# Residual steps at the end of four stages: last three weight pieces by token halves, and both residual halves ahead of the next splits

## What is computed

```
# block 1
mixed = (g_conv * y_conv + g_attn * y_attn) @ w_o
x = x + gt1 * rms_norm(mixed, g_post_mix)              # end of stage "w_o"
h = rms_norm(x, g_pre_ffn) * (1 + sc2) + sh2
f = (silu(h @ w_gate) * (h @ w_up)) @ w_down
x = x + gt2 * rms_norm(f, g_post_ffn)                  # end of stage "w_down"
# block 2
proj = rms_norm(x, norm_mix_pre) @ w_in_2 ...
x = x + rms_norm(concat(a, c) @ w_out_2, norm_mix_post)  # end of stage "w_out_2"
hn = rms_norm(x, norm_ffn_pre)
f = (silu(hn @ w_gate_2) * (hn @ w_up_2)) @ w_down_2
x = x + rms_norm(f, norm_ffn_post)                     # end of stage "w_down_2", the output
```

## Time and profile before

| | us |
|---|---|
| time, median of 3 runs | 2622.82 |
| lowest and highest of them | 2622.46, 2627.53 |
| the profiled execution, its own time | 2625.36 |
| its span, first to last instruction | 2623.6 |
| TensorE busy | 2570.8 (98% of the span) |
| DVE busy | 1688.5 (64%) |
| ACT busy | 1278.8 (49%) |
| mean granted TensorE clock | 0.995 of full speed |

### The profile page before, as it was taken

The page is one execution under the profiler, slowest core; times in us unless marked ns, Lnnn a source line. Parts: engine busy times, 40 slices in busy tenths (PEclk is TensorE's granted clock), DMA queues, the critical chain, the costliest instruction groups (busy, mean ns, idle before and its releaser), DMA issues.

```text
span 2623.6 us, 28987 instructions
## 1 busy us (share of the span) xinstructions
PE 2570.8 (98%) x11654; PEld 2101.7 (80%) x11654; DVE 1688.5 (64%) x1937; ACT 1278.8 (49%) x1775; POOL 3.9 (0%) x11
## 2 busy tenths in 40 slices
PE   7999999999999999999999999999999999999998
PEld 5788778878878888888888787788788888888886
DVE  7999899989875555555555645666655454445455
ACT  4445677754454444444444545554544444444443
POOL 0000000000000000000000000000000000000000
PEclk9999999999999999999999999999999999999999
DMA  9998466877946556666555454445455555555553
GB/s 373 358 350 311 156 222 211 292 285 287 372 182 214 206 215 240 240 225 225 202 199 185 169 191 162 171 167 195 166 194 184 191 208 191 193 188 184 190 192 129
DMA packets 80425, 578.14 MB, mean 220 GB/s; under 512 B 8974, under 2 KB 8982, under 8 KB 10529
## 3 DMA queue, kind: packets, MB, share of 16 engines
q1 hardware_dynamic: 78768, 566.92, 59.3%
q10 hardware_dynamic: 1010, 6.67, 0.6%
q0 software_dynamic: 512, 2.69, 0.3%
HBM read 574.13 MB, written 3.68 MB: 220 GB/s over the span
## 4 chain that ended last, share of the span: by engine, by line
PE 87%; DVE 5%; ACT 3%; DMA 3%; issue 1%; DVEq 0%; ACTq 0%; SPq 0%
PE bank L688 83%; DVE wlo L1528 2%; DMA raw<-in_w_o 1%; PE bank L640 1%; ACT whi L1013 1%; DMA raw<-in_w_in 1%; DVE X L1523 1%; DVE raw L1538 1%; PE bank L800 0%; ACT SS L1189 0%; PE bank L726 0%; PE bank L783 0%; PE bank L934 0%; DVE SC L1685 0%; PE bank L848 0%
## 5 line engine op out<-in xcount | busy, mean ns | idle before, releaser
L1528 DVE TENSOR_TENSOR wlo<-raw,whi 128x1024 fp32r<-128x1024 f32 x882 | 1074.2, 1224 | 882.6 <-ACT whi L1013 879.3
L1013 ACT ACTIVATE whi<-raw 128x1024 fp32r<-128x1024 f32 x882 | 931.0, 1058 | 1248.5 <-PE bank L688 1118.7
L688 PE MATMUL bank<-whi,HTh 128*128 128x512 f32 x2560 | 703.8, 397 | 7.9 <-ACT HTh L1013 5.9
L688 PE MATMUL bank<-wlo,HTh 128*128 128x512 f32 x2560 | 687.7, 390 | 5.9 <-DVE wlo L1528 5.9
L688 PE MATMUL bank<-whi,HTl 128*128 128x512 f32 x2560 | 689.0, 391 | 0.1
L688 PEld LDWEIGHTS bank<-wlo,HTh 128*128 128x128 f32 x2560 | 480.8, 188 | 110.0 <-DVE wlo L1528 8.7
L688 PEld LDWEIGHTS bank<-whi,HTl 128*128 128x128 f32 x2560 | 482.2, 189 | 104.7 <-DVE HTl L1523 1.3
L688 PEld LDWEIGHTS bank<-whi,HTh 128*128 128x128 f32 x2560 | 471.6, 189 | 106.6 <-issue 10.6
L1538 DVE CUSTOM_DVE_ANT_0 raw<-raw,GT,VECS 128x2048 f32<-128x2048 f32 x96 | 225.0, 2347 | 2.5 <-DMA raw<-in_w_ada 2.5
L688 PE MATMUL bank<-whi,ACTh 128*128 128x512 f32 x704 | 192.3, 394 | 0.0
L688 PE MATMUL bank<-wlo,ACTh 128*128 128x512 f32 x704 | 190.4, 391 | 0.0
(11 more groups left out here) (227 smaller groups left out, 1198.7 us busy)
## 6 DMA issues: line engine op xcount, KB each, us to landing
raw<-in_w_in SPq DMA_DIRECT2D x128, 1024.0 KB, 4.9
raw<-in_w_ada SPq DMA_DIRECT2D x96, 1024.0 KB, 6.5
raw<-in_w_gate SPq DMA_DIRECT2D x88, 1024.0 KB, 4.8
raw<-in_w_up SPq DMA_DIRECT2D x88, 1024.0 KB, 4.8
raw<-in_w_down SPq DMA_DIRECT2D x88, 1024.0 KB, 4.8
raw<-in_w_o SPq DMA_DIRECT2D x16, 1024.0 KB, 7.2
raw<-in_w_out SPq DMA_DIRECT2D x16, 1024.0 KB, 4.8
raw<-in_w_attn_out SPq DMA_DIRECT2D x8, 1024.0 KB, 4.8
```

Of the source, the lines that this page charges most:

```text
L688: i = e.matmul(bank[2 * ch.st + t][:, :], (xl if ps == 1 else xh)[:, k, tk(t)], (lo if ps == 2 else hi)[:, j * 512:j * 512 + 512], start=c ...
L1013: return e.activation(dst, src, ACT.Copy, scale=scale)
L1528: e.tensor_tensor(lo, src, r32(hi), S_).then_inc(lo_done, 1)
```

## The change

1. TensorE does the last three pieces of each of the four stages by token halves: half 0 of L-2, L-1 and L (then `pe_t0`), half 1 of L-2, L-1 and L, each of the last three with its `pe_done`.
2. ACT does residual half 0 in slot L-1, ahead of rounding L+1, and residual half 1 in slot L, ahead of rounding L+2.
3. DVE does both residual halves in slot L-1, ahead of subtraction L+1. All three subtractions L+1, L+2 and L+3 now stand between residual half 1 and the next norm.
4. For n = 0, half 1: ACT takes half 0's second root ahead of squaring half 1's columns, and DVE makes half 0's diagonal and the multiplication with the gain row ahead of the mean, where the mean came first. The list of DVE's steps is put in that order.

```
@@ order of DVE's steps, n = 0 @@
-    ... "quad0", (0, 0), "sum1", "mean1", "minv0", "dg0", "inv1", ...
+    ... "quad0", (0, 0), "minv0", "dg0", "sum1", "mean1", "inv1", ...
@@ tensor, piece(s) @@
-            if ch.apart and s == ch.p1 - 1:
+            if ch.apart and ch.p1 - 2 <= s < ch.p1:
                 half(s, 0)
                 return
             if ch.apart and s == ch.p1:
                 half(s, 0).then_inc(pe_t0, 1)
-                half(s - 1, 1).then_inc(pe_done, 1)
-                half(s, 1).then_inc(pe_done, 1)
+                for d in (2, 1, 0):
+                    half(s - d, 1).then_inc(pe_done, 1)
                 return
@@ scalar, residual(n, t) @@
-            evict(aparts[n], (t,))
             if n == 0 and t:
                 root(0, rr_mod[:, 0:1], res_dve[0]("quad0"), "mroot0")
+            evict(aparts[n], (t,))
@@ scalar, slots @@
+            if s + 1 in last_of:
+                residual(last_of[s + 1], 0)
             if s in last_of:
-                residual(last_of[s], 0)
-            if s - 1 in last_of:
-                residual(last_of[s - 1], 1)
+                residual(last_of[s], 1)
@@ vector, residual(n, t) @@
-            mean(n, rr, n, t, sq_act[n](3, t), "")
-            if t == 0 or n == 0:
-                late(n, t)
             if (n, t) == (0, 1):
                 diagonal(0)
+                late(n, t)
+            mean(n, rr, n, t, sq_act[n](3, t), "")
+            if t == 0:
+                late(n, t)
@@ vector, slots @@
-            if s in last_of:
-                residual(last_of[s], 0)
-            if s - 1 in last_of:
-                residual(last_of[s - 1], 1)
+            if s + 1 in last_of:
+                for t in R(2):
+                    residual(last_of[s + 1], t)
```

More of the change, by code:

```diff
@@ L434, in build @@
     JT = QT
-    res_dve = [steps("res0_dve", ["sum0", "mean0", "inv0", "xsum0", "msum0", "lin0", "quad0", (0, 0), "sum1", "mean1",
-                                  "minv0", "dg0", "inv1", "xsum1", "msum1", "lin1", "quad1", (0, 1), "minv1", "dg1",
+    res_dve = [steps("res0_dve", ["sum0", "mean0", "inv0", "xsum0", "msum0", "lin0", "quad0", (0, 0), "minv0", "dg0",
+                                  "sum1", "mean1", "inv1", "xsum1", "msum1", "lin1", "quad1", (0, 1), "minv1", "dg1",
                                   *QT[2:]])]
```

## The result

The changed kernel takes 2631.89 us (median of 8 runs, 2629.2 to 2634.47), the kernel before 2625.08 in the same comparison (8 runs, 2621.38 to 2627.53). The ratio is 1.0026, with a 95% interval of 1.0018 to 1.0035: **slower by 6.8 us**. The prediction had +6.0 us, but put it on the first three runs of before (2622.82) and not on a base that eight runs put 2.3 higher; the time lies 0.09 us above the range.

What follows compares the result with a forecast made beforehand. The bound was DVE, working in its given order, finishing the first `HTl` at the stage ends. Terms 1.25 + 0.6 + 2.3 - 0.45 = +3.7 us, plus +2.3 for the clock, gave +6.0, 2628.8 us; range 2625.3 to 2631.8.

Steps and rivals of the forecast that it cites:

- the median of the three runs is 2.54 lower, and I put the difference on the median: Base of the forecast: differences taken against the profiled 2625.36 us, then put on the three runs' median, 2.54 lower.
- The sum of the change, +6.0: Whole kernel: +3.7 us from DVE's order plus +2.3 us from the clock; as the summed case, chance 0.50.
- The order, +3.7: DVE's order at the four stage ends: `w_o` +1.25, `w_down` +0.6, `w_out_2` +2.3, `w_down_2` -0.45 us.
- 1.25 later: At `w_o`, three subtractions ahead of `HTl` instead of one make `HTl` 1.25 us later.
- the "0" for the chain up to the addition: At `w_o`, L's later end and the removed subtraction cancel up to residual half 1's addition: 0, with 0.3 either side.
- The clock, +2.3: New stall puts off the clock's return: last two passes at half speed at `w_o` and `w_out_2`, together +2.3 us.
- the upper bound of 5.1: Upper bound of the clock term, +5.1 us: the next piece too is slow in two places, 1.4 each.
- a new stall between the passes puts the return off: At the first three ends, stalls of 1.2, 1.9 and 1.8 us between first and second pass could delay the clock's return.
- Case B: Rival: the clock comes back where it did, only DVE's order costs, +3.7 us, 2626.5; chance 0.33.
- Case C: Rival: the subtractions are no cost, only gains remain, -2.2 us, 2620.6, or 2618.7 with the clock early; chance 0.07.
- Case D: Rival: half 0 not early at `w_down` and `w_down_2`, +0.5 in each; 2632 with slow next pieces; chance 0.10.
- What would show it: Signs: two more subtractions before `HTl`, its release 1.2, 0.6, 2.3 later, line 1633 behind TensorE's end, clock 0.50 throughout L+1.

Runs made afterwards that it cites:

- order_only: The changed kernel with TensorE's edit taken back, so only the last two pieces by token halves: 2630.77 us, +5.3 us against before.
- low_between: The changed kernel, but DVE takes subtraction L+1 between the two residual halves: 2627.89 us, +3.9 us against before.
- lows_behind: The changed kernel, with DVE's subtractions L+2 and L+3 behind the first quarter of the next norm: 2623.08 us, ratio 0.9994 to before.
- before_l3_behind: The kernel before, with DVE's subtraction L+3 alone moved behind the first quarter of the next norm: 2623.64 us, ratio 0.9993.
- the filled kernels: after_filled and before_filled: the changed kernel and the kernel before, with extra matmuls where TensorE would wait; +0.5 and -0.3 us against before.
- after_fill_t: The changed kernel with eight extra matmuls between the two halves' transposes only, at each of the first three ends: 2629.99 us, +5.0 us against before.
- after_filled: The changed kernel with extra unused matmuls, eight between the halves' transposes and seven between L+1's first and second pass: 2626.49 us, +0.5 us against before.
- before_filled: The kernel before with extra unused matmuls, eight between the halves' transposes and three between the passes: 2624.97 us, -0.3 us against before.

## Why the prediction was right or wrong

**The time** fell out of the range by 0.09 us. The step that failed is "the median of the three runs is 2.54 lower, and I put the difference on the median". Eight runs of before have a median of 2625.08, within 0.3 of the profiled execution's 2625.36; with three runs spread over 5 us the base was uncertain by 2 us, and the range, 3.5 down and 3.0 up from the forecast, held none of that. On a base of 2625.08 the same sum gives 2631.1, and the same range takes in 2631.89. The sum of the change, +6.0, against +6.8 measured (4.7 to 9.2 by the interval), stood. That it came so near is in part luck, for its larger term was too large, and something else made up for it.

**The order, +3.7, was too large.** By the traces it is +0.55, +0.36, +2.05 and -0.4, together 2.5. At `w_o` "1.25 later" was 0.55: three subtractions in a row take 3.49 us, not 3.67, and residual half 1's chain was 0.3 shorter than I had it; the "0" for the chain up to the addition was in truth a gain. At `w_down` and `w_out_2` the 0.2 of the three subtractions is nearly the whole miss. The mechanism held at each place: two more subtractions between addition and `HTl`, the release by DVE, `HTh` not what is waited for, `pe_t0` at `w_o` held by the wait for the weights (1.23 against 1.22 us before). order_only, low_between and lows_behind each moved one thing and moved the gap as this reading says, within 0.4 us at `w_down` and `w_out_2`; before_l3_behind did not at `w_down`, where the first pass at 1.2 GHz was the limit. The Trainium skill, page "TensorE: Matmul & The Clock Gate", section "Architectural detail: the array is 16× 32×32, not 1× 128×128", says that ACT and DVE are strict FIFO. The traces agree: in the changed kernel the subtractions of L+2 and L+3, which no pass of L+1 needs, are done ahead of the `HTl` for which TensorE stands.

**The clock, +2.3,** is neither confirmed nor refuted in its size. What the order leaves of the total is 4.3 us (2.2 to 6.7 by the interval); the filled kernels give 3.8 to 6.0, uncertain by some 3.5; the mean granted clock leaves room for 2.9, give or take 2.6. In this one pair of executions the last two passes took only 0.3 longer in all. I had costed eight matmuls at half speed at two ends, and nothing at `w_down`, because the one execution before showed all eight slow there already. But the clock varies from one execution to the next: its mean lies between 0.991 and 0.995 in the eight of the changed kernel, and one profile shows one draw of it. Whether the upper bound of 5.1 holds is open too. The reasoning, that a new stall between the passes puts the return off, held at two of three ends: counted from the start of the second pass, the clock came back after 4.4 us at `w_down` (4.0 in the kernel before) and after 3.0 at `w_out_2` (1.3 in the kernel before), but at `w_o` it was back ahead of that pass (in the kernel before 1.1 behind its start). With the sentence of the Trainium skill, page "TensorE: Matmul & The Clock Gate", Part 1, that I set beside it, "the default state is throttled, and activity releases the throttle", the trace agrees at those two ends. after_fill_t shows what the prediction did not have: the new wait can also bring the fall itself.

**The rivals.** Case B (the order alone): its +3.7 is below the interval, and the order alone is by the traces no more than 2.5; after_filled wins 6.3 us with all gaps as they were. Case C: the subtractions are a cost, in every trace. Case D: half 0 was early where it was said to be. At `w_down` its sum (line 1633) ran at 1475.90, 4.1 us ahead of TensorE's end, where it had run 2.7 ahead, and L's weights were there in time. **What would show it**: of the signs named, the release by DVE, line 1633 behind TensorE's end and the two more subtractions came; the clock was at 0.50 throughout both passes at `w_down`, mostly at `w_out_2`, but not at `w_o`.

What is still open: how large the clock's part is within some 2 to 5 us, and how it divides over the three ends, which would need many profiled executions of each kernel.

## What to carry to other kernels

Count what stands ahead of the instruction that the idle engine waits for, in the order of the engine that gives it; work that is not needed for some us goes behind it, and work that can run in a wait stays in the wait. When TensorE has to stand, a wait inside its first busy stretch can cost more than its length, for what follows may run at 1.2 GHz (in after_fill_t eight matmuls took 3.5 to 3.8 us behind it, where they take 2.0 to 2.1 at full clock). A few matmuls into an unused bank can hold the clock. They cost time where it has fallen already and they outlast the wait, and in the kernel before they won nothing that could be measured. And put a forecast on a base that was measured as often as the result will be: here three runs were 2.3 us off eight.

## What I had not expected of the hardware

Extra work made the changed kernel faster: 45 more matmuls, 6.3 us less, with every gap unchanged. In after_fill_t the granted clock fell in a wait of some 2.5 us between two passes. The same eight matmuls took 2.10 us (after_filled, `w_down`) or 3.71 us (before_filled, `w_o`), by whether the clock had fallen just before them; the second cost 2.2 us at `w_o` of before_filled. And three DVE subtractions of 1.22 us in a row took 3.49 us, 0.09 less at each seam.
